# A transformer stack on one core: bias read backwards, low halves signalled by pairs, stage entries reordered

## The chip, the cores and the metric

The kernel runs on one core of one Trainium2 chip. The metric is the device time of one execution in microseconds. Before the change the median of three runs is 2583.01 us (2581.47 to 2585.11).

## What is computed

Two stacks follow each other on a sequence of 512 tokens of width 1024, batch 1, all in float32. The first has 16 meta tokens in front (528 columns) and two layers, `h = h + layer(rms_norm(h, g))`. The second has two rounds of feed-forward, mixer, feed-forward:

```python
def layer_ab(h, w_in, w_out, rel_bias, ...):  # layer 0: indexed sparse attention and gated linear attention
    z = h @ w_in
    # oa: softmax(q k + rel_bias[bucket(j - i)] + mask of the top-k scores) v, gated
    # ob: gated linear attention in chunks of 64, head norm, gated
    return jnp.concatenate([oa, ob], axis=-1) @ w_out

def layer_cd(h, w_in, w_out, ...):            # layer 1: retention and stick-breaking attention
    oc = head_layer_norm(retention_chunked(...)) * jax.nn.silu(cg)
    od = stick_breaking(...) * jax.nn.silu(dg)
    return jnp.concatenate([oc, od], axis=-1) @ w_out

for layer in range(2):                        # second stack
    x = x + 0.5 * swiglu(rms_norm_2(x, ffn1_norm[layer]), ...)
    hn = rms_norm_2(x, mix_norm[layer])
    x = x + (pool_mla_mixer(hn, ...) if layer % 2 == 0 else gated_conv_mixer(hn, ...))
    x = x + 0.5 * swiglu(rms_norm_2(x, ffn2_norm[layer]), ...)
```

with `swiglu(x) = (silu(x @ w_gate) * (x @ w_up)) @ w_down`, hidden width 2816, and `rms_norm(x, g) = x * rsqrt(mean(x * x) + 1e-6) * g`. The first stack ends in a further `rms_norm` with `final_g`.

## The kernel before

**State and blocks.** The activations stay transposed in SBUF as `H`: 128 channels on the partitions, 8 tiles (m or k = 0 to 7) of 528 or 512 tokens. All large products go through 219 weight blocks of 256 columns and up to 8 k-tiles of 128 rows (172 have 8, 24 have 4, 16 have 6). A block is loaded by SP into `raw` (two buffers, `load_block`, L443), rounded by ScalarE in one operation to its high half `wh` (`split_high`, L458), and POOL makes the low half `wl = raw - wh` in one operation for each two k-tiles (`split_low`, L468), up to four per block, and signals `weights_low` after the last. The activations are split in the same way into a high part `NH` by ScalarE and a low part `NL` by VectorE. TensorE then makes each product as three matmuls (high by high, high by low, low by high; `gemm_k`, L482). A block gives two output units of 128 rows and 512 columns (or two column halves of 264, line L493; or five token tiles, line L503), k running inside a unit.

**Order.** Every engine's order is written out by hand; engines wait for counting semaphores alone, in program order, so whatever stands behind a waiting instruction on an engine waits too. TensorE waits for the whole block's `weights_low` before its first unit. SP's loads wait until the block two before is consumed by POOL; `split_high` of block b waits until TensorE has finished block b - 2.

**PSUM.** Units without a bank of their own take bank `unit % 4`; `wait_slot` (L476) waits for the eviction of the unit that held the bank. Banks 4 to 7 serve the attentions, the sums of squares and the transposes.

**Entries.** The norm of a stage is put off: the products of a stage run on `H * g` and are scaled by 1/rms at eviction. So an entry into a stage (ab, cd, ffn0, mla, ffn1, ffn2, conv, ffn3) runs beside the end of the stage before. For each finished tile m VectorE adds the unit into `H` (L2320, L2322 or L1072), `late_act` (L563) makes the high part and the square on ScalarE, `late_dve` (L583) the low part (L590) and the sum of squares over tiles in `rstd` (L597; for ffn0 a second sum, weighted with `final_g`, in `both`, L596). `late_sum_pe` (L607) sums over the partitions on TensorE after the first unit of the new stage, and `late_root_act` (L623) and `late_scale_dve` (L636) make root and reciprocal (3.36 us for 512 columns on VectorE). `split_high` of the new stage's first two blocks stands among the `late_act` calls on ScalarE's queue (`out_tail_act` L2328, `ffn_act` L1028).

**Start.** SP loads the meta tokens, the constants, block 0, the four tiles of x, block 1 and small tables. TensorE transposes the meta tokens, then the gain rows (ten DMAs on ScalarE's queue), then x (32 transposes, L2530); ScalarE and VectorE evict them into `H`. The first two blocks run in two halves of k, so that they can begin before all input tiles are split.

**Bias of the sparse attention.** A line of 655 relative-position biases per head is written to HBM and read back with overlapping rows into `strip` (128 rows, each shifted by one). The rows come out mirrored over the partitions, and `strips_pe` (L1749) turns them with a matmul against `flip`, one head at a time in two column halves; `strips_act` (L1758) evicts them. POOL adds strip and mask into `bm` (L2382), VectorE adds `bm` to the scores (L910). `soft_pe` (L812) runs the steps i of an attention: transposes of the probabilities (`turn`), the next scores, values, and `fill(i)`, which is a number of k-steps of other blocks put in to keep TensorE busy (8 for i = 0 and 1 in the sparse attention, 1 in the latent attention). VectorE's list (`soft_dve`) runs beside it, with one round of the top-k selection in each of the first steps.

## Time and profile before

| | |
|---|---|
| median of three runs | 2583.01 us |
| profiled execution | 2583.35 us, span 2581.5 us |
| TensorE busy | 2500.5 us, 97% |
| POOL / VectorE / ScalarE busy | 1074.2 / 1018.9 / 872.5 us |
| chain that ended last | 88% TensorE, 5% VectorE, 3% ScalarE, 2% POOL |
| weights' low halves on POOL (L473) | 794 operations of 1346 ns |
| mean DMA rate | 84 GB/s |

Busy time says which engine is full; here TensorE nearly is, and what it loses has to be looked up place by place: in the view of waits (what TensorE waited for and how often), in the chain of work around each such place, and in the order of time of one engine. Mean durations come from the view that groups instructions by line and shape. A matmul's recorded duration covers its latency; the pace is the distance between starts. PEclk is the granted share of TensorE's 2.4 GHz.

### The profile page before, as it was taken

What the parts mean: (1) busy time and instruction counts of PE and PEld (TensorE: products, weight loads), DVE (VectorE), ACT (ScalarE), POOL (GpSimd) and SP (SyncE); (2) the same over time, 40 slices, a digit from 0 to 9 for tenths busy, and PEclk for the clock granted to TensorE, in tenths of its full rate; (3) what the DMA queues carried; (4) which work ended last, traced back from release to release, by engine and by line L of the source; (5) the groups of instructions that cost most, each with busy time, mean ns of one, the idle gap of its engine ahead of it and who ended that gap; (6) DMA issues with size and microseconds to landing.
All of it is one profiled execution on the core that took longest, in us unless ns stands there. A gap on an engine that the chain in (4) does not pass through costs nothing.

```text
span 2581.5 us, 31377 instructions
## 1 busy us (share of the span) xinstructions
PE 2500.5 (97%) x13015; PEld 2058.3 (80%) x13015; DVE 1018.9 (39%) x1663; ACT 872.5 (34%) x1294; POOL 1074.2 (42%) x830
## 2 busy tenths in 40 slices
PE   7999899999989999999999999999999999999999
PEld 6899768876668888878678888788888788888887
DVE  3666345235573131357452221531222544422222
ACT  4423444336642222235542222322222322322221
POOL 3233244331145444443154444444444444444443
PEclk9999999999999999999999999999999999999999
DMA  4122103211033333222133333233232333232322
GB/s 134 58 74 72 47 23 107 82 50 33 25 101 98 98 98 98 82 80 64 34 98 98 98 99 98 90 100 102 86 102 89 102 98 98 94 102 86 103 89 82
DMA packets 215847, 217.73 MB, mean 84 GB/s; under 512 B 10599, under 2 KB 213090, under 8 KB 215706
## 3 DMA queue, kind: packets, MB, share of 16 engines
q1 hardware_dynamic: 215504, 215.68, 26.3%
q8 instruction: 103, 1.69, 0.3%
q14 instruction: 38, 0.31, 0.0%
q10 hardware_dynamic: 202, 0.06, 0.0%
HBM read 213.60 MB, written 2.12 MB: 84 GB/s over the span
## 4 chain that ended last, share of the span: by engine, by line
PE 88%; DVE 5%; ACT 3%; POOL 2%; issue 1%; DMA 1%; ACTq 0%; DVEq 0%; SPq 0%
PE ps L500 68%; PE ps L493 6%; PE ps L503 4%; PE ps L497 2%; POOL wl L473 2%; PE ps L828 2%; ACT wh L466 1%; PE ps L863 1%; PE ps L845 1%; DVE rstd L597 1%; PE ps L2097 1%; PE ps L1585 1%; PE ps L522 0%; DMA raw<-in_w_in_ab 0%; DVE NL L590 0%
## 5 line engine op out<-in xcount | busy, mean ns | idle before, releaser
L473 POOL TENSOR_TENSOR wl<-raw,wh 128x512 fp32r<-128x512 f32 x794 | 1044.3, 1346 | 1453.1 <-ACT wh L466 1453.0
L500 PE MATMUL ps<-NH,wh 128*128 128x512 f32 (+1 forms) x1824 | 718.6, 394 | 21.5 <-POOL wl L473 14.1
L500 PE MATMUL ps<-NL,wh 128*128 128x512 f32 (+1 forms) x1824 | 712.9, 391 | 0.0
L500 PE MATMUL ps<-NH,wl 128*128 128x512 f32 (+1 forms) x1824 | 712.1, 390 | 0.0
L466 ACT ACTIVATE wh<-raw 128x2048 fp32r<-128x2048 f32 (+4 forms) x219 | 380.6, 1738 | 462.3 <-PE ps L500 404.2
L500 PEld LDWEIGHTS ps<-NH,wh 128*128 128x128 f32 (+1 forms) x1824 | 343.4, 188 | 102.8 <-POOL wl L473 17.4
L500 PEld LDWEIGHTS ps<-NL,wh 128*128 128x128 f32 (+1 forms) x1824 | 343.3, 188 | 73.7 <-issue 1.7
L500 PEld LDWEIGHTS ps<-NH,wl 128*128 128x128 f32 (+1 forms) x1824 | 343.3, 188 | 73.2
L500 PE MATMUL ps<-GH,wh 128*128 128x512 f32 x824 | 323.1, 392 | 0.0
L500 PE MATMUL ps<-GH,wl 128*128 128x512 f32 x824 | 320.7, 389 | 0.0
L500 PE MATMUL ps<-GL,wh 128*128 128x512 f32 x824 | 320.7, 389 | 0.0
L1072 DVE SCALAR_TENSOR_TENSOR H<-ps,H 128x512 f32<-128x512 f32 x96 | 66.4, 691 | 327.3 <-PE ps L500 327.0
L1039 ACT ACTIVATE GH<-tmp 128x512 fp32r<-128x512 f32 x88 | 55.7, 633 | 375.0 <-DVE tmp L1065 375.0
L500 PEld LDWEIGHTS ps<-GH,wh 128*128 128x128 f32 x824 | 154.7, 188 | 33.0 <-issue 1.2
L500 PEld LDWEIGHTS ps<-GH,wl 128*128 128x128 f32 x824 | 154.7, 188 | 32.3
L500 PEld LDWEIGHTS ps<-GL,wh 128*128 128x128 f32 x824 | 154.7, 188 | 31.5
L1035 ACT ACTIVATE sg<-sg 128x512 f32<-128x512 f32 x88 | 55.6, 633 | 316.2 <-DVE sg L1056 316.2
L1056 DVE TENSOR_TENSOR sg<-ps,rstd 128x512 f32<-128x512 f32 x66 | 45.7, 692 | 236.5 <-PE ps L500 236.4
L1062 DVE TENSOR_TENSOR tmp<-ps,rstd 128x512 f32<-128x512 f32 x66 | 45.7, 692 | 211.9 <-PE ps L500 211.9
L1067 DVE TENSOR_TENSOR GL<-tmp,GH 128x512 fp32r<-128x512 f32 x88 | 73.4, 834 | 61.6 <-ACT GH L1039 61.6
L1065 DVE TENSOR_TENSOR tmp<-sg,tmp 128x512 f32<-128x512 f32 x88 | 90.1, 1024 | 3.0
L503 PE MATMUL ps<-wh,NH 128*128 128x256 f32 (+1 forms) x320 | 90.7, 283 | 0.3 <-ACT dv L1777 0.3
(416 smaller groups left out, 2958.7 us busy)
## 6 DMA issues: line engine op xcount, KB each, us to landing
raw<-in_ffn_w_gate SPq DMA_DIRECT2D x44, 1024.0 KB, 5.3
raw<-in_ffn_w_up SPq DMA_DIRECT2D x44, 1024.0 KB, 5.3
raw<-in_ffn_w_down SPq DMA_DIRECT2D x32, 1024.0 KB, 5.1
raw<-in_w_in_ab SPq DMA_DIRECT2D x16, 1024.0 KB, 5.5
raw<-in_w_in_cd SPq DMA_DIRECT2D x14, 1024.0 KB, 5.0
raw<-in_ffn_w_down SPq DMA_DIRECT2D x16, 768.0 KB, 4.4
raw<-in_c_w_in SPq DMA_DIRECT2D x12, 1024.0 KB, 5.2
raw<-in_w_out_ab SPq DMA_DIRECT2D x8, 512.0 KB, 3.5
```

What stands on the lines that cost most here:

```text
L466: nc.scalar.activation(wh[:, b % 2, 0:k, 0:w], raw[:, b % 2, 0:k, 0:w], ACT.Copy).then_inc(S("weights_high"), 1)
L473: ins = nc.gpsimd.tensor_tensor(wl[:, b % 2, ks, 0:w], raw[:, b % 2, ks, 0:w], wh[:, b % 2, ks, 0:w].bitcast(F32), ALU.subtract)
L493: last = nc.tensor.matmul(ps[0:m1 - m0, bank + h, 0:T // 2], w[:, s, k, m0:m1], x(k)[:, h * (T // 2):(h + 1) * (T // 2)], start=start, sto ...
L497: last = nc.tensor.matmul(ps[:, bank, 0:T // 2], w[:, s, k, m0:m0 + P], x(k)[:, c0:c0 + T // 2], start=start, stop=stop)
L500: last = nc.tensor.matmul(ps[0:m1 - m0, bank, 0:SEQ], w[:, s, k, m0:m1], x(k), start=start, stop=stop)
L503: last = nc.tensor.matmul(ps[0:n_tok, bank, 0:total], x(k)[:, c0:c0 + n_tok], w[:, s, k, 0:total], start=start, stop=stop)
L828: last = nc.tensor.matmul(ps[0:n, A.score_bank(i) + x, 0:min(w - 512 * x, 512)], A.q(h, c0, n), A.k(h, 512 * x, min(w - 512 * x, 512)), st ...
L1035: nc.scalar.activation(sg[:, i, :], sg[:, i, :], ACT.Silu).then_inc(S("gate_silu"), 1)
L1039: nc.scalar.activation(GH[:, 2 * p_ + i, :], tmp[:, i, 0:SEQ], ACT.Copy).then_inc(S("hidden_high"), 1)
L1065: nc.vector.tensor_tensor(tmp[:, i, 0:SEQ], sg[:, i, :], tmp[:, i, 0:SEQ], ALU.mult).then_inc(S("hidden"), 1)
L1067: nc.vector.tensor_tensor(GL[:, 2 * p_ + i, :], tmp[:, i, 0:SEQ], GH[:, 2 * p_ + i, :].bitcast(F32), ALU.subtract).then_inc(S("hidden_low" ...
L1072: nc.vector.scalar_tensor_tensor(out=H[:, m, META:T], in0=ps[:, bank_of(u), :], scalar=0.5, in1=H[:, m, META:T], op0=ALU.mult, op1=ALU.add ...
```

## The change

- **Strips.** The table of buckets is mirrored on the host, `flip` and both strip routines are gone, and each use reads `strip` backwards along its columns (step -1). TensorE waits only for the value units' evictions before the attention. SP loads block ag+1 ahead of the strip.
- **Signals per pair.** POOL signals `weights_low` after each pair of k-tiles, and TensorE waits in a block's first unit pair by pair.
- **Entries.** `late_act` and `late_dve` are cut into high part, square, low part and add. On ScalarE the split of the next blocks goes ahead of the squares, on VectorE the adds run a tile behind the low parts. Except in ab and cd the squares are written to PSUM banks 6 and 7 (and 4 and 5 for ffn0's second ones). ffn0's sum goes behind the second unit, and its second reciprocal behind the first two evictions.
- **Banks.** `unit % 4` becomes `(unit + 2) % 4`; kv_up and q_up follow.
- **Fill.** `fill(0)` runs ahead of step 0.
- **Start.** x is loaded ahead of block 0, and block 0 in two halves; the gain rows are transposed after x; ScalarE splits block 0 in two operations after its evictions; the squares of ab come after all high parts, their adds after all low parts.

```diff
-    out["flip"] = np.eye(P)[::-1]
-    return (np.arange(32)[:, None] == b[None, :]).astype(np.float32)
+    return np.ascontiguousarray((np.arange(32)[:, None] == b[None, ::-1]).astype(np.float32))
-            bank = b.bank[i] if b.bank else unit % 4
+            bank = b.bank[i] if b.bank else (unit + 2) % 4
@@ split_low
         for k0 in range(0, k, 2):
+            if b == 0 and k0 % 4 == 0:
+                pool.wait_ge(S("weights_high" if k0 else "first_high"), 1)
             ks = slice(k0, min(k, k0 + 2))
-            ins = nc.gpsimd.tensor_tensor(wl[:, b % 2, ks, 0:w], ..., ALU.subtract)
-        ins.then_inc(S("weights_low"), 1)
+            nc.gpsimd.tensor_tensor(wl[:, b % 2, ks, 0:w], ..., ALU.subtract).then_inc(S("weights_low"), 1)
@@ unit_steps, gemm
-            pe.wait_ge(S("weights_low"), b + 1)
             wait_slot(pe, BLOCKS[b].unit0 + i)
             for k in range(BLOCKS[b].kts):
+                if i == 0 and k % 2 == 0:
+                    pe.wait_ge(S("weights_low"), low_count(b, k))
                 gemm_k(pe, b, i, k, hi, lo)
-            if i == 0 and sums:
+            if sums and i == (sums == "ffn0"):
                 late_sum_pe(pe, sums)
@@
+    def late_square_at(name, m):
+        return tmp[:, m % 2, 0:T] if name in ("ab", "cd") else ps[:, 6 + m % 2, :]
+    def late_pair_act(act, name, q, b):
+        late_high(act, name, 2 * q)
+        if q:
+            late_square(act, name, 2 * q - 1)
+        if q < KT // 2 - 1:
+            split_high(act, b)
+            late_high(act, name, 2 * q + 1)
+            late_square(act, name, 2 * q)
+        else:
+            late_high(act, name, KT - 1)
+            split_high(act, b)
+            late_square(act, name, KT - 2)
+            late_square(act, name, KT - 1)
@@ late_scale_dve, ffn_dve
             step(dve, nc.vector.reciprocal(both[:, :], both[:, :]))
-            dve.wait_ge(S("norm_root"), roots_before[name] + 2)
+            return
+                    if p_ == 0:
+                        dve.wait_ge(S("norm_root"), roots_before["ffn0"] + 2)
+                        step(dve, nc.vector.reciprocal(rstd[:, 0:SEQ], rstd[:, 0:SEQ]))
@@ soft_pe
         scores(1)
+        A.fill(0)
         for i in range(N):
-            if A.fill:
+            if i:
                 A.fill(i)
@@ strips
+    def strip_of(h, at_, n, w):
+        a = strip[0:n, h, T - 1 - at_:T - at_]
+        return bass.AP(a.tensor, a.offset, [list(a.ap[0]), [-1, w]])
-            return strip[0:n, h, 400:400 + w]
+            return strip_of(h, 400, n, w)
-        strips_pe(pe)
-        pe.wait_ge(S("strip_out"), HEADS)
+        pe.wait_ge(S("evac_act"), evacs_before(FIRST["ag"], "A"))
@@ out_tail_dve (ffn_dve in the same manner, without the lag of the low part)
             if m:
-                late_dve(dve, after, m - 1)
-        late_dve(dve, after, KT - 1)
+                late_low(dve, after, m - 1)
+            if m >= 2:
+                late_add(dve, after, m - 2)
+        late_low(dve, after, KT - 1)
+        late_add(dve, after, KT - 2)
+        late_add(dve, after, KT - 1)
@@ sync
-        load_block(sp, 0)
         for t in range(NT):
             sp.dma_start(xt[:, t, :], inp["x"][0, t * P:(t + 1) * P, :]).then_inc(S(f"x_in_{t}"), 16)
+        for h in range(2):
+            src = inp["w_in_ab"][0][h * D // 2:(h + 1) * D // 2, ...].rearrange("(k p) c -> p k c", p=P)
+            sp.dma_start(raw[:, 0, 4 * h:4 * h + 4, :], src).then_inc(S("raw_ready_0" if h else "raw_first"), 16)
+        load_block(sp, FIRST["ag"] + 1)
         sp.wait_ge(S("bias_stored"), 16)
         sp.wait_ge(S("gla_mix_low"), NT + 1)
         sp.dma_start(strip[:, :, :], ...)
@@ scalar
-        split_high(act, 0)
         for t in range(NT): ...                # evictions of x
+        split_first_high(act, 0)
         act.wait_ge(S("gain_done"), 1)
-        late_act(act, "ab", 0)
-        late_act(act, "ab", 1)
+        late_high(act, "ab", 0)
+        late_high(act, "ab", 1)
+        split_first_high(act, 1)
+        late_high(act, "ab", 2)
+        late_high(act, "ab", 3)
         split_high(act, 1)
-        for m in range(2, KT):
-            late_act(act, "ab", m)
+        for m in range(4, KT):
+            late_high(act, "ab", m)
+        for m in range(KT):
+            late_square(act, "ab", m)
```

## Rows read from the trace of the kernel before

**Rows 1.** the page's busy shares, and the chain of work: start us, us, what

```profile
PE 2500.5 (97%) x13015; PEld 2058.3 (80%) x13015; DVE 1018.9 (39%) x1663; ACT 872.5 (34%) x1294; POOL 1074.2 (42%) x830
...
1681.53 341.45 PE ps L500 x1506
```

**Rows 2.** TensorE's waits in the whole span: us in total, times, longest

```profile
PE ps L500 <- POOL wl L473: 15.1, 9, 2.6
```

**Rows 3.** the chain of work in the first 48 us

```profile
10.84 5.36 PE ps L2530 x32
...
34.72 11.29 PE ps L500 x48
```

**Rows 4.** the instructions on tile xt, with first and last start in us

```profile
L2342 SPq DMA_DIRECT2D xt<-in_x x4: 432/513/1067, 2.1 to 3.7; - x4
...
DMA to landing us min/median/max: 7.6/8.8/10.0
```

**Rows 5.** TensorE in order of time: start us, us, instruction [idle before, releaser]

```profile
18.39 0.47 PE L500 MATMUL ps<-NH,wh 128*128 128x512 f32 x1 [2.20 <-DVE NL L590]
18.70 0.40 PE L500 MATMUL ps<-NL,wh 128*128 128x512 f32 x1
```

**Rows 6.** by line and shape: count | busy us, mean ns | idle before

```profile
L473 POOL TENSOR_TENSOR wl<-raw,wh 128x512 fp32r<-128x512 f32 x783 | 1034.9, 1352 | 1436.1 <-ACT wh L466 1436.1
...
L466 ACT ACTIVATE wh<-raw 128x2048 fp32r<-128x2048 f32 x170 | 324.2, 1907 | 419.7 <-PE ps L500 367.2 <-PE ps L493 40.1 <-PE ps L497 9.2
...
L597 DVE TENSOR_TENSOR rstd<-rstd,tmp 128x512 f32<-128x512 f32 x42 | 47.2, 1123 | 0.0
...
L2322 DVE TENSOR_TENSOR H<-ps,H 128x512 f32<-128x512 f32 x24 | 16.5, 687 | 35.1 <-PE ps L500 31.9 <-PE ps L522 3.1
...
L2382 POOL TENSOR_TENSOR bm<-strip,score 128x528 f32<-128x528 f32 x8 | 10.9, 1358 | 12.4 <-DVE mx L910 12.4
```

**Rows 7.** chain, then TensorE and VectorE in order of time, around the strips

```profile
249.93 11.53 DMA raw<-in_w_in_ab
...
259.56 1.94 PE L1755 MATMUL ps<-strip,K 128*128 128x264 f32 x8
265.36 8.21 PE L1755 MATMUL ps<-strip,K 128*128 128x264 f32 x24 [3.86 <-ACT strip L1762]
...
275.58 0.52 PE L493 MATMUL ps<-NH,wh 128*128 128x264 f32 x2
...
282.67 0.48 PE L493 MATMUL ps<-NH,wh 128*128 128x264 f32 x2 [0.72 <-DVE agT L1746]
...
276.65 0.69 DVE L1691 MAX8 top<-score 128x8 f32<-128x528 f32 x1
```

**Rows 8.** VectorE and TensorE in order of time, entry into cd

```profile
413.44 0.71 DVE L2320 TENSOR_TENSOR H<-ps,H 128x528 f32<-128x528 f32 x1 [0.92 <-PE ps L493]
...
420.75 1.79 DVE L590 SCALAR_TENSOR_TENSOR NL<-H,gain,NH 128x528 fp32r<-128x528 f32 x1
422.46 1.79 DVE L597 TENSOR_TENSOR rstd<-rstd,tmp 128x528 f32<-128x528 f32 x1
...
424.35 1.19 PE L614 MATMUL ps<-K,rstd 128*16 128x1 f32 x10
```

**Rows 9.** the chain of work, entry into ffn0

```profile
720.79 5.93 PE ps L500 x24
...
762.20 3.36 DVE both L645
...
778.80 1.43 PE ps L500 x5
```

**Rows 10.** chain at ffn1 and ffn2, and ffn1's window: busy us, PEclk, DMA

```profile
1311.36 7.31 PE ps L500 x24
...
1674.92 5.76 PE ps L500 x24
...
1311.00:1315.00 4.00, 3.64 (x9) 2.89 (x10) 4.00 (x3) 2.33 (x3) 4.00 (x4) 0.57 0.58 172
```

More of the change, by code:

```diff
@@ L192, in weight_plan @@
         blocks.append(Block(("a_w_in_2", 0), (0, D), cols, "DD"))
[L193 to L194 removed]
+    add("kv_up", "a_w_kv_up_2", 0, 0, 256, 0, 1024, "A", "T0", [2, 3, 0, 1] * 4)
+    add("q_up", "a_w_q_up_2", 0, 0, 384, 0, 768, "A", "T0", [2, 3, 0, 1] * 3)
     add("out_pool", "a_w_out_2", 0, 0, D // 2, 0, D, "D", "F", [2, 3, 2, 3, 2, 3, 2, 3])
@@ L237, in bank_of, with low_count @@
     return UNITS[u][2]
+LOW_BEFORE = [0]
+for _blk in BLOCKS:
+    LOW_BEFORE.append(LOW_BEFORE[-1] + -(-_blk.kts // 2))
+def low_count(b, k):
+    return LOW_BEFORE[b] + k // 2 + 1
 def program(nc, inp, const_in, buckets_in, out, bias_line):
@@ L544, in gemm @@
             for k in range(blk.kts):
+                if i == 0 and k % 2 == 0:
+                    pe.wait_ge(S("weights_low"), low_count(b, k))
                 if i == 0 and ready:
@@ L595, in late_dve @@
             if name == "ffn0":
-                nc.vector.tensor_tensor(both[:, :], both[:, :], sg[:, m % 2, :], ALU.add)
-            ins = nc.vector.tensor_tensor(rstd[:, 0:w], rstd[:, 0:w], tmp[:, m % 2, 0:w], ALU.add)
+                nc.vector.tensor_tensor(both[:, :], ps[:, 4 + m % 2, :], both[:, :], ALU.add)
+            ins = nc.vector.tensor_tensor(rstd[:, 0:w], late_square_at(name, m), rstd[:, 0:w], ALU.add)
             if name == "ffn0" and m == KT - 1:
@@ L603, in late_dve @@
             if name == "ffn0":
-                nc.vector.tensor_copy(both[:, :], sg[:, 0, :])
-            nc.vector.tensor_copy(rstd[:, 0:w], tmp[:, 0, 0:w]).then_inc(S("square_added"), 1)
+                nc.vector.tensor_copy(both[:, :], ps[:, 4, :])
+            nc.vector.tensor_copy(rstd[:, 0:w], late_square_at(name, 0)).then_inc(S("square_added"), 1)
     def late_sum_pe(pe, name):
@@ L1074, in ffn_dve @@
                 if t0 == GROUPS[-1][0] and AFTER[f]:
-                    late_dve(dve, AFTER[f], m)
+                    late_low(dve, AFTER[f], m)
+                    if m:
+                        late_add(dve, AFTER[f], m - 1)
+            if t0 == GROUPS[-1][0] and AFTER[f]:
+                late_add(dve, AFTER[f], KT - 1)
     def ffn_pe(pe, f):
@@ L1747, in ab_dve @@
                                        in1=halves(rstd[0:n, :], T), op0=ALU.mult, op1=ALU.mult).then_inc(S("evac_dve"), 1)
-    def strips_pe(pe):
-        pe.wait_ge(S("side_in"), 32)
-        for h in range(HEADS):
-            if h >= 2:
-                pe.wait_ge(S("strip_out"), h - 1)
-            for x in range(2):
-                last = nc.tensor.matmul(ps[:, 2 + 2 * (h % 2) + x, 0:halfT], const("flip"), strip[:, h, x * halfT:(x + 1) * halfT], start=True, stop=True)
-            last.then_inc(S("strip_turned"), 1)
-    def strips_act(act):
-        nc.scalar.preload_act_table_set("natural_log_exp_and_others")
-        for h in range(HEADS):
-            act.wait_ge(S("strip_turned"), h + 1)
-            nc.scalar.activation(halves(strip[:, h, :], T), banks(2 + 2 * (h % 2), T), ACT.Copy).then_inc(S("strip_out"), 1)
     def cd_name(b):
@@ L2355, in _ @@
         sp.dma_start(strip[:, :, :], bass.AP(bias_line.tensor, bias_line.offset, [[1, P], [BIAS_SPAN, HEADS], [1, T]])).then_inc(S("side_in"), 16)
-        for b in range(FIRST["ag"] + 1, C0 + 2):
+        for b in range(FIRST["ag"] + 2, C0 + 2):
             load_block(sp, b)
@@ L2381, in _ @@
                 pool.wait_ge(S("unit_done"), units_before(OG))
-            nc.gpsimd.tensor_tensor(bm_of(i)[:, 0:w], strip[:, h, at_:at_ + w], score[:, SCO[t - 1]:SCO[t - 1] + w], ALU.add).then_inc(S("bias_masked"), 1)
+            nc.gpsimd.tensor_tensor(bm_of(i)[:, 0:w], strip_of(h, at_, P, w), score[:, SCO[t - 1]:SCO[t - 1] + w], ALU.add).then_inc(S("bias_masked"), 1)
             if i in (9, 15, 23, 31):
@@ L2454, in _ @@
         nc.vector.tensor_copy(H[:, :, 0:META], ps[:, 4, 0:KT * META].rearrange("p (k n) -> p k n", k=KT)).then_inc(S("h_done"), 1)
-        dve.wait_ge(S("gain_turned"), 1)
-        nc.vector.tensor_copy(gain[:, 0:NROWS], ps[:, 0, 0:NROWS]).then_inc(S("gain_done"), 1)
         for t in range(NT):
@@ L2459, in _ @@
             nc.vector.tensor_copy(H[:, 0:4, META + t * P:META + (t + 1) * P], ps[:, 4 + (2 * t + 1) % 4, :].rearrange("p (k n) -> p k n", k=4)).then_inc(S("h_done"), 1)
+        dve.wait_ge(S("gain_turned"), 1)
+        nc.vector.tensor_copy(gain[:, 0:NROWS], ps[:, 0, 0:NROWS]).then_inc(S("gain_done"), 1)
         for m in range(KT):
-            late_dve(dve, "ab", m)
+            late_low(dve, "ab", m)
+        for m in range(KT):
+            late_add(dve, "ab", m)
         dve.wait_ge(S("gain_done"), 1)
@@ L2517, in _ @@
         last.then_inc(S("turned_in"), 1)
-        pe.wait_ge(S("rows_in"), 16 * len(ROWS))
-        nc.tensor.transpose(ps[:, 0, 0:NROWS], rows[:, :], ident[0:NROWS, 0:NROWS]).then_inc(S("gain_turned"), 1)
         for g in range(2 * NT):
@@ L2531, in _ @@
             last.then_inc(S("turned_in"), 1)
+        pe.wait_ge(S("rows_in"), 16 * len(ROWS))
+        nc.tensor.transpose(ps[:, 0, 0:NROWS], rows[:, :], ident[0:NROWS, 0:NROWS]).then_inc(S("gain_turned"), 1)
         pe.wait_ge(S("gain_done"), 1)
```

60 lines of the change are left out of this document (31 added, 29 removed).

## The prediction

> **What bounds the kernel now.** I read the profile in this order: busy shares, who waits for whom on TensorE, then the chain of work at each place with a wait. TensorE is busy 97% of the span of 2581.5 us, and in the long dense stretches one 512-column matmul follows another every 341.45/1506 = 0.2267 us [rows 1]. The change takes away hardly any of that arithmetic, so all it can gain is TensorE's waits, the stretches in which it runs at half clock, and the 32 flip matmuls. TensorE's waits are short and many: the longest sum is that on the low halves of the weights from POOL, 15.1 us in 9 waits, none over 2.6 [rows 2]. The reader should see that the eight entries into a new stage hold nearly all of them, and that between the entries there is nothing to gain.
>
> **Part 1, the start (inputs first, block 0 in halves, squares put off).** Before, the x tiles land 7.6 to 10.0 us after issues at 2.1 to 3.7, so at 9.7 to 13.7, 1.33 us apart, behind the 1 MB of block 0 [rows 4]. Moved ahead of it they land earlier by what that megabyte takes: two x tiles' worth is 2.7 us, and up to 4 if its small pieces are slower than x; the last x tile lands at 9.7 to 11.0. TensorE no longer waits for the gain rows in front of x either. It needs 5.36 us for the 32 transposes [rows 3], about what the landing takes, so it ends at 11.3 to 12.0 instead of 16.2: 4.5 us earlier. The gain transpose and its copy then stand behind x and ahead of the first product (0.7 us). New in front of the first product is the first half of block 0 on ScalarE (half of 1.907 us [rows 6], so 1.0) and POOL's first pair (1.35 [rows 6], up to 1.7 beside VectorE); the low part of input tile 0 runs beside POOL and takes up to 1.8, as the low parts of rows 8 do. So 12.0 + 0.6 (last eviction) + 1.0 + 0.7 (high part) + 1.5 = 15.8 for the first matmul, against 18.39 [rows 5]: 2.6 us. With the squares and their adds put off VectorE makes only low parts; one each 1.75 us against TensorE's 1.4 us per input tile of a block leaves four waits of 0.3 and 0.1 of others, where before there were two of about 1.8 and several of 0.1 (the end of the stage is 34.72 + 11.29 = 46.0 [rows 3], 27.6 us after the first matmul, for 96 matmuls of 0.23 and 1.6 us of bias line). That is 2.9 more: **-5.5** (-3.5 if x lands late, -7.2 if VectorE and POOL don't meet). The adds end near 33 us and the sum is wanted at 40, so the put-off squares are hidden here. The gain DMAs on ScalarE's queue, the rest of SP's queue and the load of block 2 (0.3 to 4 us later, because block 0's low half ends later) are hidden by block 0 and 1.
>
> **Part 2, the strips.** Before, 32 flip matmuls and eight evictions stand between the last value block (259.56) and the first fill (275.58): 16.0 us, of which 3.86 is a wait, because ScalarE is held by block ag+1, which lands 11.53 us after its issue behind the strip DMA [rows 7]. The clock falls in that wait: the last 24 flips take 8.21 us, the first 8 only 1.94 [rows 7]. After, the strip is read backwards where it is used, and block ag+1 is loaded before the strip, long before it is wanted. What remains is the wait for the last value eviction and two small score products, 1.3 us: -14.7. The moved fill gives part back. Fill 0 (5.95 us) now runs before turn 0, and fill 1 needs VectorE's eviction of fill 0's unit, which stands behind the copy of turn 0, logits 2 and one top-k round (0.69 + 0.09 + 0.69, each with its gap, 1.55 [rows 7]), all now late because they wait for turn 0; with the eviction of 0.71 fill 1 starts near 269.7, where it was 282.67 [rows 7]. **-12.9** (-10 to -14.7). POOL's reads with step -1 are not shown by any row; the adds are 1.36 us at most [rows 6] in steps of 3 us with one step of slack, so the bounds are 0 and, at three times the price, 1 us in each of the 8 widest, +8; I take 0, the row as it stands, since the number of elements is the same.
>
> **Part 3, signals per pair and the new order at the entries.** A block's low halves are four POOL operations, 5.9 us when VectorE is busy too, behind 1.9 us on ScalarE: 7.9 us after the last reader of the buffer; the block before it lasts 5.5 us at depth 4. With a signal per pair TensorE needs 1.9 + 1.5 = 3.4 us, and each later pair comes 1.5 us after, against 2.7 us of matmuls. At the depth-6 blocks in front of mla, ffn2 and conv (8.2 us) it is enough that the split stands ahead of the squares. So POOL's 15.1 us [rows 2] go, entry by entry:
> - mla, ffn2, conv: 1.9 each (the entry unit is 5.76 us [rows 10]). What is late next is the sum: last tile's eviction 0.75, high 0.65, split 1.9, two squares 1.3, then one add of 0.7 and two hand-overs, 5.4 us after the last unit, against 5.44 for the first unit of the new stage. It just fits, because the squares now lie in PSUM: an add with one PSUM operand takes 0.687 us even beside POOL (mean of 24), one with both in SBUF 1.123 on the mean of 42 [rows 6], and 1.79 beside POOL [rows 8]. -5.6, and -1.65 for the third block of mla's input, which is the same wait again.
> - ffn1: its wait of 2.6 us is followed by a stretch at 0.57 clock, so that 24 matmuls take 7.31 us instead of 5.6 [rows 10]. Both go, less 0.1: -4.2. ffn3: -0.3.
> - ffn0: two units from 720.79 are 5.5 us; eight units of 2.78 end at 743.4, two blocks of 10.9 and the two sums at full clock (1.7) with 0.7 for a late low part bring the third block at 768, where it was 778.80 [rows 9]. Putting the sum behind the second unit, both square sums in PSUM and the second reciprocal (3.36 [rows 9]) behind the first evictions make that reachable: sum at 755.3, root, one reciprocal, silu, split and pair end near 766.5, under the 768. **-10.9** (-8 if low parts beside POOL cost 1.8 each, -11.5).
> - cd: here the squares stay in SBUF and the split stands ahead of the last two. Before, VectorE has a queue without a gap from 413.44 to 424.25, and TensorE's sum starts just behind it at 424.35 [rows 8]. After, one more add lies behind the seventh tile and the last two squares come 2 us later: split ends 420.9, squares 422.1, two adds of 1.75: 425.0. TensorE has done its first unit by 421.8, so 2.4 us won become a wait of 3.2, +0.8. Waits of 2.6 and 3.86 us are followed by half clock [rows 7, 10]; I take 1.7 us for that: **+2.6** (-2.4 if VectorE keeps up, +4.5).
> - mla attention: one fill step (0.7 us) goes under the wait for the first exponentials: -0.7 (0 to -1.2).
> - Bank rotation: an entry's first units take the banks of four units before instead of two; no row waits for a bank there, 0.
> - The added waits are 575 on TensorE (one per pair instead of one per block). In the unit of [rows 10] eight satisfied waits leave 5.76 us for 24 matmuls, 23 steps of 0.2267 and one duration of 0.5, so 0 each; 0.005 at most, +3.
>
> The Trainium skill's page "SBUF — State Buffer", section "SBUF: two separate sides", says that a VectorE operation with two SBUF inputs and a GpSimd operation exclude each other for the whole instruction. The durations 0.69 and 1.79 agree. By that rule a blocked add costs up to a whole POOL operation of 1.35 more, 2.05, which would put 0.5 us on cd and make the sum -38.9. It speaks against splitting weights just when cd's adds run.
>
> **The sum**: -5.5 - 12.9 - 5.6 - 1.65 - 4.2 - 0.3 - 10.9 + 2.6 - 0.7 = **-39.2 us**. The profiled execution took 2583.35 us, 1.85 around its span; the median of the runs is 2583.01. So 2544.2 for that execution and 2543.8 for the median.
>
> **The rivals.**
> (a) The wait moves: the put-off squares end after the first unit at every entry. Then POOL's place is taken by the sum. If a PSUM operand spared nothing, each of five entries would wait 2 us (+10) and ffn0's six late adds would give back 4: 2558. A milder form (1 us each, half clock after two) gives +8: 2552. For it: cd's queue. Against: 0.687 us. Chance 0.15.
> (b) Slower: a satisfied wait on TensorE is not free. It decides from 39.2/575 = 0.068 us each. After a real wait the second matmul comes 18.70 - 18.39 = 0.31 us later instead of 0.23 [rows 5]; at 0.1 per wait the change costs 57: 2601. Against it stand the eight waits of rows 10. Chance 0.03.
> (c) The edits do more: cd's adds keep up (-5), fill 1 doesn't wait (-1.8), start -7: 2535. Chance 0.17.
> (d) The edits at the start and at the strips don't do what they say: x lands as late as before because its place in the queue doesn't set when it lands (-2 instead of -5.5), or reading backwards is three times as dear (+8): 2547 to 2555. Chance 0.10.
>
> **How the numbers follow.** Forecast 0.55, between 2540 and 2549 by the bounds of cd, ffn0 and the start; (a) 0.15, (b) 0.03, (c) 0.17, (d) 0.10. To leave out no more than 2 in 10 the range takes all of (d), the milder (a) and the upper half of (c): 2536 to 2555. A measurement of this kernel can tell 0.2% (5 us) from no change. Of the cases (b) alone is slower; with what I may have missed, faster 0.95, same 0.02, slower 0.03.
>
> **What would show it.** x transposed by 12 us and the first product near 15.8; no flip matmuls and full clock from 260 to 283; fill 1 waiting 2 us for VectorE; no wait on POOL at an entry; cd's sum waiting 3 us with half clock after it; ffn0's third block 11 us nearer to the stage's start; 0.2267 us per matmul in the dense stretches. A longer step there, or waits for the sum at mla, ffn1, ffn2 and conv, would make the prediction wrong.

## The result, and the profile after

The changed kernel takes 2541.89 us (median of four runs, 2540.93 to 2543.49), the kernel before 2582.98 beside it: a ratio of 0.9841, with a 95% interval from 0.9824 to 0.9858. That is 41.1 us less; the prediction said 39.2 less and 2543.8. The profiled execution has a span of 2540.6 us, against 2581.5. Times of variants below are medians of three to five executions; one execution of the variant with the warm start took 3108.64 us at a granted clock of 0.75 and is left out.

First TensorE's waits in the whole span (columns as in [rows 2]). The nine waits on POOL, 15.1 us, are gone, and only one has taken their place at an entry, the 2.4 us at the sum of cd. Of the waits that are left, the one for the constants at the very start (4.6 us, before 4.4) and the four at L2153 in stick-breaking (6.5 together, before 6.8) stand outside the change. Three single ones are what the rest of this text comes back to: 3.5 in front of the first product, 1.9 at fill 1, 2.4 at the sum of cd.

```profile
PE ps L2153 <- DVE soft_lo L2250: 6.5, 4, 1.9
...
PE ps L516 <- DVE NL L624: 3.5, 1, 3.5
PE ps L509 <- DVE agT L1797: 2.7, 3, 1.9
PE ps L653 <- DVE rstd L636: 2.4, 1, 2.4
```

The page and the chain of work of after. TensorE's busy time fell by only 11.9 us, to 98% of the span. The dense stretch is as dense as in [rows 1]: 359.09/1584 = 0.2267 us per matmul, with the added waits in it.

```profile
PE 2488.6 (98%) x12983; PEld 2053.7 (81%) x12983; DVE 999.4 (39%) x1663; ACT 866.2 (34%) x1287; POOL 1069.4 (42%) x830
...
1642.86 359.09 PE ps L516 x1584
```

The chain of work at the start of after, and the landing of the x tiles (answer to [rows 3 to 5]). x lands 4.3 to 6.9 us after its issues, where it was 7.6 to 10.0; the transposes end at 12.23, the first product starts at 15.85, and the first 48 matmuls take 13.90 us.

```profile
6.03 6.20 PE ps L2576 x32
...
14.45 1.27 DVE NL L624
...
15.85 13.90 PE ps L516 x48
```

```profile
DMA to landing us min/median/max: 4.3/5.6/6.9
```

Windows of after (busy us of PE, PEld, DVE, ACT, POOL with their instructions, then PEclk, DMA share, GB/s). Right behind the first product, behind fill 1 and behind the sum of cd the granted clock is half (0.50, 1.2 GHz). In the last row, where the stick-breaking stage begins, it is full, which will matter below.

```profile
14.60:21.30 6.70, 5.45 (x13) 4.32 (x14) 6.70 (x5) 6.70 (x9) 6.70 (x5) 0.50 0.13 34
...
264.00:267.00 3.00, 2.84 (x13) 2.84 (x14) 1.66 (x7) 0.65 (x1) 0.00 (x0) 0.50 0.29 103
...
407.20:413.80 6.60, 6.60 (x22) 5.51 (x20) 2.01 (x3) 0.70 (x3) 2.14 (x2) 0.50 0.47 159
...
562.90:569.50 6.60, 6.41 (x39) 4.69 (x40) 4.67 (x12) 5.35 (x16) 3.11 (x3) 1.00 0.34 113
```

TensorE and VectorE of after at the strips (answer to [rows 7]). The flip matmuls are gone. Fill 0 runs from 255.3 to 261.3; fill 1 waits 1.92 us for the eviction of L1797, and before that eviction stand a copy, the logits and one top-k round (MAX8 and MATCH_REPLACE8), just as the prediction had it.

```profile
255.14 0.22 PE L867 MATMUL ps<-akT,aqT 64*16 64x16 f32 x4 [0.66 <-ACT av L1770]
...
261.86 0.69 DVE L1742 MAX8 top<-score 128x8 f32<-128x528 f32 x1
...
262.67 0.69 DVE L1743 MATCH_REPLACE8 score<-top,score 128x528 f32<-128x528 f32 x1
263.39 0.71 DVE L1797 SCALAR_TENSOR_TENSOR agT<-ps,rstd 128x528 f32<-128x528 f32 x1
...
264.16 0.81 PE L509 MATMUL ps<-NH,wh 128*128 128x264 f32 x2 [1.92 <-DVE agT L1797]
```

By line and shape (answer to [rows 6]). The square sums at 512 columns take 681 ns, where they took 1123. The bias adds that read the strip backwards take 1357 ns, where the forward ones took 1358.

```profile
L636 DVE TENSOR_TENSOR rstd<-ps,rstd 128x512 f32<-128x512 f32 x42 | 28.6, 681 | 5.7 <-ACT ps L602 5.1
...
L2423 POOL TENSOR_TENSOR bm<-strip,score 128x528 f32<-128x528 f32 x8 | 10.9, 1357 | 12.4 <-DVE mx L950 12.4
```

The chain at the entry into ffn0 (answer to [rows 9]): 144 matmuls without a break, the four sum matmuls, and 353.65 us without a break. Second unit, square sums, root and reciprocal delay nothing.

```profile
704.48 33.54 PE ps L516 x144
738.02 0.86 PE ps L658 x2
738.88 0.86 PE ps L659 x2
739.74 353.65 PE ps L516 x1560
```

Where the time went: the start of the same TensorE instruction in both traces, and what each stretch gained (negative is faster).

| mark | before | after | difference | this stretch | predicted |
|---|---|---|---|---|---|
| index stage, second step | 63.77 | 59.99 | -3.8 | -3.8 | -5.5 |
| end of the value blocks | 259.56 | 254.48 | -5.1 | -1.3 | 0 |
| fill 1 | 282.67 | 264.16 | -18.5 | -13.4 | -12.9 |
| last spread of the sparse attention | 390.87 | 373.63 | -17.2 | +1.3 | 0 |
| cd, behind its entry | 461.86 | 447.76 | -14.1 | +3.1 | +2.6 |
| last suffix sums of stick-breaking | 660.54 | 644.24 | -16.3 | -2.2 | 0 |
| mla input, after the sum | 1124.78 | 1094.32 | -30.5 | -14.2 | -12.8 |
| latent projections | 1198.33 | 1166.09 | -32.2 | -1.8 | -1.65 |
| last spread of the latent attention | 1284.81 | 1252.11 | -32.7 | -0.5 | -0.7 |
| ffn1 | 1319.60 | 1282.80 | -36.8 | -4.1 | -4.2 |
| ffn2 | 1681.61 | 1642.92 | -38.7 | -1.9 | -1.9 |
| conv | 2043.59 | 2003.05 | -40.5 | -1.9 | -1.9 |
| ffn3, and to the end | 2219.09 | 2178.20 | -40.9 | -0.4 | -0.3 |

### The profile page after: what moved, and what is told of

Same layout as the page of the kernel before. It is cut to its first block, busy times and chain, and to the rows that moved or that the text cites. A ratio compares the mean times of both kernels' runs of the same rounds, so it can differ in the third digit from the quotient of the medians.

```text
span 2540.6 us, 31320 instructions
## 1 busy us (share of the span) xinstructions
PE 2488.6 (98%) x12983; PEld 2053.7 (81%) x12983; DVE 999.4 (39%) x1663; ACT 866.2 (34%) x1287; POOL 1069.4 (42%) x830
## 4 chain that ended last, share of the span: by engine, by line
PE 94%; DVE 3%; ACT 2%; issue 1%; DMA 0%; DVEq 0%; SPq 0%; ACTq 0%
PE ps L516 72%; PE ps L509 6%; PE ps L519 5%; PE ps L513 2%; PE ps L867 2%; PE ps L902 1%; PE ps L884 1%; ACT wh L475 1%; PE ps L2133 1%; PE ps L1636 1%; PE ps L538 0%; PE ps L1999 0%; PE ps L1979 0%; DVE rstd L636 0%; PE ps L2191 0%
## 5 line engine op out<-in xcount | busy, mean ns | idle before, releaser
L475 ACT ACTIVATE wh<-raw 128x2048 fp32r<-128x2048 f32 (+3 forms) x218 | 378.8, 1738 | 477.7 <-PE ps L516 425.2
```

What stands on the lines that cost most here:

```text
L475: nc.scalar.activation(wh[:, b % 2, 0:k, 0:w], raw[:, b % 2, 0:k, 0:w], ACT.Copy).then_inc(S("weights_high"), 1)
```

## The experiments

All are edits of the changed kernel, except where the kernel before is named, and the changed kernel's 2541.9 us is what they stand against. Each was timed beside the kernel before. The runs of one kernel lie 1 to 8 us apart, so each verdict rests first on the trace at its place, and the median stands beside it.

**The start: TensorE kept busy.**

```diff
+        for _ in range(16):
+            nc.tensor.transpose(ps[:, 1, 0:P], xt[:, 3, 0:P], ident)
         pe.wait_ge(S("gain_done"), 1)
         ready = late_ready(pe, "ab")
```

> The changed kernel with 16 transposes of an x tile into an unused bank between the gain transpose and the first product, so that TensorE isn't idle for 3.5 us there. Theory (the idle stretch from 12.3 to 15.85 us brings the half clock of 14.56 to 21.38, and that eats what the start should have gained): full clock from 11 us on, the first product still at 15.85, the first 48 matmuls in 10.9 us plus about 1 us of waits for low parts instead of 13.9; 2.0 us less than the changed kernel (2541.9), so 2539.9. Rival (the half clock is bound to the time since the start, or the low parts would have kept TensorE waiting all the same): 2541.9, first 48 matmuls 13.9 us as now.

TensorE at its first product, then the chain at the third input tile and windows of this kernel:

```profile
15.15 0.47 PE L516 MATMUL ps<-NH,wh 128*128 128x512 f32 x1 [1.79 <-DVE NL L624]
```

```profile
18.59 8.84 PE ps L516 x36
27.43 0.95 PE ps L2596 x2
```

```profile
13.80:20.40 6.60, 5.10 (x19) 3.34 (x20) 6.60 (x5) 6.32 (x8) 6.60 (x5) 1.00 0.30 89
559.30:565.80 6.50, 6.33 (x24) 3.96 (x25) 4.79 (x11) 5.32 (x16) 3.07 (x3) 0.50 0.38 115
```

The clock is full in the first window, and the first 48 matmuls take 27.43 - 15.15 = 12.3 us instead of 13.9: 1.6 less. But the time is 2542.12 us (2541.34 to 2542.57): the same as without the edit. The traces show two reasons.

First, the changed kernel's profiled run had drawn the dear case. Ten profiled runs, of the changed kernel and of nine variants, keep the idle gap of 3.5 us. Three of them have 6.8 us of half clock at the start (48 matmuls in 13.9 to 14.0 us), six have 3.4 us (12.7 to 13.0), and one, the variant further down that reads the strip forwards, has none (19.56 + 8.83 - 16.13 = 12.3 us). Its first product, then its chain and a window:

```profile
16.13 0.47 PE L516 MATMUL ps<-NH,wh 128*128 128x512 f32 x1 [3.54 <-DVE NL L624]
```

```profile
19.56 8.83 PE ps L516 x36
```

```profile
14.00:20.80 6.80, 4.53 (x17) 3.14 (x18) 6.07 (x4) 6.74 (x10) 6.65 (x5) 1.00 0.26 75
```

So half clock follows the gap in nine runs of ten, and in neither of the two runs (this one and the one with three edits) in which the gap is filled up to its last 1.8 us. That the idle stretch brings it is likely, but it doesn't bring it every time, and filling it is worth 0 to 1.6 us, 0.9 on the mean of the ten.

Second, half clock comes and goes elsewhere. At the beginning of stick-breaking, behind waits of 1.56 and 0.84 us that stand in both traces, this run has 6.8 us of half clock (the second window), and the changed kernel's profiled run has none (its window 562.90:569.50, the same work, above); in retention this run has 3.4 us less. Of the twelve profiled runs of the changed kernel and its variants, six show half clock at the beginning of stick-breaking, for 3.4 or 6.8 us, and six show none. The profiled run is 1.1 us shorter than the changed kernel's, and the medians can't tell the edit from nothing.

**Fill 1: the eviction ahead of the top-k round.**

```diff
@@ dsa_between
-        if eng is dve_e[0] and i <= LATE_ROUNDS:
-            next(dsa.rounds, None)
         for n, end in enumerate(DSA_ENDS):
             ...
+        if eng is dve_e[0] and i <= LATE_ROUNDS:
+            next(dsa.rounds, None)
```

> The changed kernel with VectorE's eviction of the fill units ahead of the top-k round in each step of the sparse attention instead of behind it. Theory (fill 1 waits 1.92 us because the eviction stands behind one top-k round of 1.5 us, and the half clock of 263.73 to 267.14 comes from that wait): the wait falls to 0.4 us, no half clock there, 1.5 + 1.7 = 3.2 us less: 2538.7. Rival (the round then makes the next probabilities late, and the wait moves to turn 1 or 2): 2541.9, the 1.9 us at another place of the same steps.

```profile
260.79 0.52 PE L509 MATMUL ps<-NH,wh 128*128 128x264 f32 x2 [0.38 <-DVE agT L1796]
```

```profile
262.00:266.00 4.00, 4.00 (x35) 4.00 (x34) 0.44 (x4) 0.50 (x1) 0.00 (x0) 1.00 0.21 74
```

In TensorE's timeline the wait is 0.38 us instead of 1.92, and the window behind it has full clock. From the first scores to the last spread the attention takes 115.5 us instead of 118.5, 3.0 less. Measured 2539.97 (2537.32 to 2540.76): 1.9 less. The theory holds, and no later turn waits longer.

**Fill 0 back behind turn 0**, as before the change.

```diff
         scores(1)
-        A.fill(0)
         for i in range(N):
             turn(i)
             ...
-            if i:
+            if A.fill:
                 A.fill(i)
```

> The changed kernel with fill 0 back behind turn 0 in both attentions. Theory (the moved fill covers the 3.1 us from the first scores to the first probabilities, 255.4 to 258.5, and gives 1.9 back as the wait of fill 1 for VectorE): 3.1 - 1.9 = 1.2 us more at the sparse attention, 0.7 more at the latent attention (its first wait 1.2 us again instead of 0.5), half clock in either: 2543.8. Rival (the move loses more than it covers, because the eviction behind the round is its doing): 2541 or less.

```profile
260.30 0.19 PE L881 MATMUL ps<-K,lg 16*16 16x16 f32 x1 [3.20 <-ACT lg L1035]
```

TensorE's timeline shows the 3.20 us that the moved fill covers, and fill 1 waits 0.63 instead of 1.92. The half clock after it lasts from 259.2 to 266.0, twice as long as in the changed kernel, so the attention takes 2.8 us more, not 1.2; the latent attention takes 0.6 more. Measured 2547.20 (2544.69 to 2549.59), 5.3 more. The sign is the theory's, the size is not: 3.4 stand at the two places. The profiled run is 7.1 us longer; the rest of that is half clock elsewhere, at 61.2, 566.4 and 1139.8 us (3.4 us each), against 3.4 us less of it at cd.

**cd: the sum behind the second unit.**

```diff
-            if sums and i == (sums == "ffn0"):
+            if sums and i == (sums in ("ffn0", "cd")):
```

> The changed kernel with the sum of squares of cd behind the second unit of its first block, as ffn0 has it. Theory (VectorE's last two adds beside POOL end at 407.0, 2.4 us after TensorE's first unit, and that wait costs 3.4 us more as half clock from 407.09 to 413.92): the wait of 2.4 us and the half clock both go, 5.8 us less: 2536.1. Rival 1 (the half clock there is not due to the wait): 2.4 less, 2539.5. Rival 2 (root and reciprocal of 3.4 us, now 1.5 us later after the sum, hold up the evictions and so the banks of the third block): the gain is given back there, 2541 to 2542.

```profile
421.18 0.48 PE L509 MATMUL ps<-NH,wh 128*128 128x264 f32 x2 [1.99 <-DVE cqT L1837]
```

The wait of 2.4 and its half clock are gone, but TensorE now waits 1.99 us at the third block for VectorE's eviction of cd's first unit, with 3.4 us of half clock behind it. The stretch from the last spread to the mark of cd takes 72.2 us instead of 74.1. Measured 2539.09 (2538.26 to 2544.02), 2.8 less. The second rival has the mechanism right: the sum is what the evictions wait for, and a bank of the first block is what TensorE needs next. It had the whole gain given back, and 1.9 us are left at the place.

**cd: the last four squares in PSUM.**

```diff
     def late_square_at(name, m):
+        if name == "cd" and m >= 4:
+            return banks(4 + 2 * (m % 2), T)
```

> The changed kernel with the squares of cd's last four tiles in PSUM banks 4 to 7, which are free by then. Theory (the adds of 1.8 and 1.5 us beside POOL are what makes cd's sum late): adds of 0.7 us, the sum waits under 0.3 us instead of 2.4, no half clock from 407 to 414: 5.8 us less, 2536.1. Rival (the sum is late because its last squares stand behind the split on ScalarE, whatever the adds cost): 0.9 us of wait or more is left, and half clock after it: 2539.5.

VectorE's last two adds, first of the changed kernel and then of this one, and a window of this one over the sum:

```profile
403.93 3.06 DVE L636 TENSOR_TENSOR rstd<-tmp,rstd 128x528 f32<-128x528 f32 x2 [0.74 <-ACT tmp L602]
```

```profile
401.65 1.52 DVE L641 TENSOR_TENSOR rstd<-ps,rstd 128x528 f32<-128x528 f32 x2 [0.23 <-ACT ps L607]
```

```profile
404.00:412.00 8.00, 8.00 (x43) 6.82 (x43) 5.22 (x7) 1.59 (x4) 2.29 (x2) 1.00 0.56 184
```

Two adds beside POOL take 1.52 us together, where they took 3.06. TensorE doesn't wait at all, the clock stays full, and the stretch takes 68.45 us instead of 74.13: 5.7 less, as the theory had it. The median is 2539.93 (2538.27 to 2543.24), only 2.0 less; the profiled run has gained 4.1 and again shows the half clock at stick-breaking (556.1 to 562.9) and 3.4 us of it at 460.5, where the changed kernel's had none.

**Where the squares lie, in all entries.** Here every square goes to `tmp`, and ffn0's second ones to `sg`.

```diff
     def late_square_at(name, m):
-        return tmp[:, m % 2, 0:T] if name in ("ab", "cd") else ps[:, 6 + m % 2, :]
+        return tmp[:, m % 2, 0:T if name in ("ab", "cd") else SEQ]
```

> The changed kernel with all squares of the late norms in SBUF (as cd has them), nothing else. Theory (an add with one operand in PSUM takes 0.68 us even beside POOL, one with both in SBUF up to 1.8; the sums just fit because of that): L636 between 0.7 and 1.8 us each, up to 1.1 us more wait for the sum at each of mla, ffn1, ffn2, conv, ffn3, and 2 at ffn0: 2 to 8 us more, 2546 as the middle. Rival (a PSUM operand spares nothing, or there was slack): adds as now and 2541.9.

Waits on TensorE, the adds by shape, and the chain at ffn1, of this kernel:

```profile
PE ps L659 <- DVE rstd L636: 10.0, 5, 2.8
```

```profile
L636 DVE TENSOR_TENSOR rstd<-tmp,rstd 128x512 f32<-128x512 f32 x42 | 48.8, 1161 | 6.5 <-ACT tmp L602 6.0
```

```profile
1281.33 1.70 DVE rstd L636
1283.03 0.61 DVE H L2358
...
1284.29 1.91 ACT wh L475
...
1286.75 1.37 DVE rstd L636
...
1288.22 1.58 DVE rstd L636
...
1289.84 2.08 PE ps L659 x2
```

Measured 2560.11 (2559.32 to 2560.57): 18.2 more, over twice the upper end of what I expected. TensorE waits for the sum 0.9 us at mla, 2.8 at ffn1, 2.4 at ffn2 and conv and 1.5 at ffn3, together 10.0, where it was at most 0.13 us late; ffn0 has two waits for low parts, 1.5 us together; and half clock of 3.4 us, worth 1.7, follows at ffn0, ffn1 and ffn2. That is 10.0 + 1.5 + 5.1 = 16.6. Two more such stretches stand at 186.9 and 1139.2, where nothing waits longer than before, and at the start and at cd the half clock is 3.4 us shorter each. The chain shows why it is more than the 1.1 us of one slow add. An add of 1.70 us delays the last tile's addition into `H`, that delays its high part and the split, and the last two adds stand behind them: three slow adds in one chain, not one. They take 4.65 us where three of 0.68 take 2.04, and that 2.6 us is nearly all of ffn1's wait of 2.8. This is rival (a) of the prediction turned on; its 2558 is 2 us from what was measured, though ffn0 lost about 4 us and the five sums waited 2 us only on the mean.

The Trainium skill's page "SBUF — State Buffer", section "SBUF: two separate sides", says that a VectorE operation with two inputs in SBUF and a GpSimd operation that reads SBUF exclude each other for the whole instruction. The rows agree: 0.67 to 0.69 us in all 42 adds with one input in PSUM, 0.68 to 1.81 with both in SBUF.

**The kernel before with its squares in PSUM**, and nothing else.

```diff
-        nc.scalar.activation(tmp[:, m % 2, 0:w], late_src(name, m), ACT.Square)
+        nc.scalar.activation(late_square_at(name, m), late_src(name, m), ACT.Square)
```

> The kernel before with one part of the change alone: the late squares in PSUM instead of SBUF, except in ab and cd. Theory (the 18 us that the changed kernel loses with squares in SBUF are worth little here, because at mla, ffn1, ffn2 and conv TensorE's wait on POOL in front of the first unit covers the late adds; only ffn0, where the sum is late already, gains): adds of 0.68 us, 2 to 6 us less than before, 2577 to 2581. Rival (the squares' place is worth its 18 us by itself): 2565.

```profile
PE ps L500 <- POOL wl L473: 12.6, 8, 2.3
```

Measured 2573.33 (2569.43 to 2574.50), a ratio of 0.9958 (0.9944 to 0.9971): 10 less. It lies between the two expectations. Eight of the nine waits on POOL stay, so at mla, ffn2 and conv the faster adds bring 0.45 us each; ffn1 gains 2.0, its wait 2.2 instead of 2.6 and without the half clock. From stick-breaking to ffn0's third block the run gains 7.6 us: the sum waits 0.71 instead of 3.12, the waits of 0.95 for POOL and 1.94 for a low part in front of it are gone, and so is the half clock of 755 to 762. With 0.5 at ffn3 that is 11.5 at the places of the edit; a half clock of 10.2 us at 63.9, where the kernel before had none, takes 4.5 back, and one stretch fewer behind it gives 1.5. The same placement is worth 10 us here and 18 in the changed kernel.

**TensorE waits for whole blocks again.**

```diff
-                if i == 0 and k % 2 == 0:
-                    pe.wait_ge(S("weights_low"), low_count(b, k))
+                if i == 0 and k == 0:
+                    pe.wait_ge(S("weights_low"), LOW_BEFORE[b + 1])
```

> The changed kernel in which TensorE waits for a block's whole low half before its first unit (outside the start), all else as changed. Theory (at depth 4 the pairs do it, since 7.8 us from the last reader to the last low half stand against 5.5 us of matmuls; at depth 6 the order of the split does it alone): about 2.5 us of wait and 1.7 us of half clock back at ffn1, up to the same at ffn0, 0 at mla, ffn2 and conv: 4 to 9 us more, 2548 as the middle. Rival 1 (the pair signals do all): 1.9 us back at each of mla, ffn2 and conv too, 12 to 15 more. Rival 2 (the order does all): 2541.9.

```profile
PE ps L516 <- POOL wl L490: 5.0, 2, 3.4
...
PE ps L516 <- DVE H L2356: 2.3, 1, 2.3
...
PE ps L516 <- issue: 2.2, 1, 2.2
PE ps L516 <- DVE H L2358: 2.1, 1, 2.1
```

Measured 2551.90 (2550.99 to 2554.76), 10.0 more. The waits are 2.3 at cd, 2.1 at ffn0, 3.4 at ffn0's third block, 1.6 at mla's third block and 2.2 at ffn1; the profile names three different releasers, but at each of these places TensorE starts 0.1 us behind the end of POOL's last pair (at ffn1 1284.41 behind 1281.36 + 2.95). At mla, ffn2 and conv there is none, so there the order of the split is enough. At cd the wait costs nothing, since the sum then waits 2.4 us less and the half clock behind it is gone too. The theory named ffn0 and ffn1 and missed the third blocks of ffn0 and mla and the wait at cd; its upper end was 9 us more.

**Squares ahead of the splits again**, pair signals kept.

```diff
@@ late_pair_act
+        late_high(act, name, 2 * q)
+        late_square(act, name, 2 * q)
+        if name in ("cd", "ffn0", "ffn1", "ffn3"):
+            split_high(act, b)
+        late_high(act, name, 2 * q + 1)
+        late_square(act, name, 2 * q + 1)
+        if name in ("mla", "ffn2", "conv"):
+            split_high(act, b)
```

> The changed kernel in which ScalarE makes each square right after its high part and splits the next block behind that, as before; pair signals, PSUM squares and VectorE's order stay. Theory (pair signals and order each do alone at depth 6; at depth 4 the pairs do it): no wait on POOL over 0.5 us at any entry, 2541 to 2543. Rival (the order is what takes the waits away): waits of 1 to 1.9 us on POOL at mla, ffn2 and conv again, 2546 to 2548.

No wait on POOL comes back at any entry, so the rival falls: either part alone takes away the waits at depth 6. Measured 2545.73 (2543.07 to 2546.27), 3.8 more and above the theory. Two waits of 0.82 and 0.70 us for low parts are new, at cd and ffn0, because there the high parts now stand behind two squares; 1.9 us more in the profiled run come with half clock from 564.5 us, where stick-breaking begins.

**Reading the strip forwards.**

```diff
     def strip_of(h, at_, n, w):
-        a = strip[0:n, h, T - 1 - at_:T - at_]
-        return bass.AP(a.tensor, a.offset, [list(a.ap[0]), [-1, w]])
+        return strip[0:n, h, T - at_ - w:T - at_]
```

> The changed kernel with the bias strip read forwards from the mirrored place, so that the bias added is another one and only the time is to be read. Theory (step -1 costs nothing: the 528-column adds took 1.3 us at the median in both kernels): L2423 and the steps of the sparse attention as they are, 2541.9. Rival (the 1.3 us that the attention took longer than before comes from the backwards reads): 1 us or more less, 2540.5, with shorter adds on POOL or shorter steps on VectorE.

```profile
L2422 POOL TENSOR_TENSOR bm<-strip,score x16: 1026/1302/1689, 320.2 to 363.0; 128x400 f32<-128x400 f32 x8, 128x528 f32<-128x528 f32 x8
```

The line gives min/median/max in ns; backwards they are 1032/1306/1685. The attention takes 118.7 us, backwards 118.5. Measured 2543.45 (2542.45 to 2549.95). Direction costs nothing that these numbers can show.

**Some 2600 waits more.**

```diff
-                if i == 0 and k % 2 == 0:
-                    pe.wait_ge(S("weights_low"), low_count(b, k))
+                pe.wait_ge(S("weights_low"), low_count(b, k))
```

> The changed kernel with a wait on the signal of the weights' low halves ahead of every k-step of every unit, not only each second one of a block's first unit: some 2600 waits more on TensorE, nearly all on a value that was reached long before. Theory (a satisfied wait is free): 2541.9 and 0.2267 us per matmul in the dense stretches, at most 0.005 us each, 2555. Rival (b of the prediction, 0.068 us each): 2720.

```profile
1641.01 359.09 PE ps L516 x1584
```

The same 359.09 us for the same 1584 matmuls, and 2542.69 us: 0.8 more, 0.0003 us for each added wait and within the scatter. Rival (b) falls.

**The three edits together**, those of the warm start, of the eviction and of cd's squares in PSUM, as shown above.

> The changed kernel with three edits: transposes that keep TensorE busy before the first product, the eviction ahead of the top-k round, cd's last squares in PSUM. Theory (the three places are independent; by the traces of the single runs 1.6 at the start, 3.0 at the strips, 5.8 at cd): 10.4 us less than the changed kernel, 2531.5. Rival (as in the run with the warm start alone, the clock falls at other waits instead, in the retention and stick-breaking stages): only 5 to 7 less, 2535 to 2537.

Measured 2534.29 us (2531.27 to 2536.32, five runs), a ratio to the kernel before of 0.9809 (0.9796 to 0.9823), and 0.9970 of the changed kernel's median. The profiled run has 2529.5 us of span, 11.1 less than the changed kernel's. By the marks of the table it is 2.2 less at the start, 3.0 at the strips and 5.7 at cd. The beginning of stick-breaking is at full clock in this run:

```profile
552.00:559.00 7.00, 7.00 (x42) 5.14 (x43) 5.19 (x12) 5.12 (x16) 2.85 (x2) 1.00 0.44 145
```

So the sum of the three shows in the profiled run, which is the fastest of the five, and 7.6 of it in the median, which lies between the theory's 2531.5 and the rival's 2535 to 2537. The slowest of the five runs is 4.6 us under the fastest of the changed kernel, so the gain is clear of noise. It is the fastest version here.

## Why the prediction was right, and where it was not

- **Part 1, the start.** x landed in 5.6 us at the median instead of 8.8, the transposes ended at 12.23 (predicted 11.3 to 12.0) and the first product came at 15.85 (15.8). The step "that is 2.9 more" failed in this run: it was 1.2 (59.99 - 15.85 = 44.1 us from the first product to the mark, before 63.77 - 18.39 = 45.4). What this step had wrong is the clock, and nothing else. The sum took full clock; what came was half clock from 14.56 to 21.38, at which one matmul takes 0.43 us and VectorE keeps up. In the two runs with full clock there, with the gap filled (57.67 - 15.15) and with the strip read forwards (58.63 - 16.13), the stretch takes 42.5 us, 2.9 less than before, and small delays for low parts like those of the sum are back, 0.3 us at the third input tile. The prediction had itself lengthened TensorE's idle time in front of the first product, from 2.2 us [rows 5] to 3.5, and applied the lesson of [rows 7] and [rows 10] (a wait, then half clock) everywhere but here. -3.8 instead of -5.5. That the earlier landing comes from the place in the queue is what the two traces suggest; no run takes the order of the loads back alone.
- **Part 2, the strips.** -13.4 against -12.9 at fill 1, its wait 1.92 against 2. Then 1.3 come back as half clock from 263.73 to 267.14. Among its signs the prediction had "full clock from 260 to 283"; that was wrong, and for the same reason. The cost of reading backwards, 0 with an upper bound of 8, is 0.
- **Part 3.** ffn2, conv and ffn1 came as predicted, to 0.1 us. That it "just fits" is true to within half a microsecond: the weight load of the sum is 0.33 to 0.55 us late in four places, 1.5 together, its matmul at most 0.13. That the PSUM operand is what makes it fit is shown by the 18 us. ffn0 with mla's entry gained 14.2 against 12.8. ffn0's third block starts at 750.5, 12.0 nearer instead of 10.9; the remaining 2.2, up to mla's sum, stand against 1.9. Part of the 1.1 is in the prediction's own sum: 720.79 + 8 x 2.78 is 743.0, not 743.4, and with two blocks, the sums and the low part that gives 767.2, not 768. Of the rest, the low part that it had waiting for 0.7 us beside POOL didn't make TensorE wait. "Against 2.7 us of matmuls" for a pair is misread as well: in a block's first unit a pair lasts 6 x 0.2267 = 1.4 us, less than the 1.5 that POOL needs. It does no harm, because the first pair is ready 2 us before TensorE wants it (3.4 against 5.5).
- **cd.** The wait was 2.40 where the sum had 3.2, and the half clock 6.8 us where it had half of that: +3.1 against +2.6. Two errors of opposite sign, so the nearness is luck (and the sum's own terms, 0.8 and 1.7, make 2.5). That slow adds beside POOL make the sum late is shown by the variant with the squares in PSUM. In the paragraph on the Trainium skill, two adds 0.26 to 0.3 us longer would make the sum -38.7, not -38.9.
- **Fill of the latent attention, ffn3, satisfied waits:** as predicted, to 0.2 us. The experiment bounds a satisfied wait far below the 0.005 us that I allowed. No wait for a bank shows in the changed kernel, but no run has the bank rotation alone.
- **Not in the sum.** -1.3 up to the strips and -2.2 in retention and stick-breaking come with two half-clock stretches fewer, each of 3.4 us and worth 1.7. Two windows of before, then one of after over the same work as the second (the one over the same work as the first is the last window at the top):

```profile
577.80:581.00 3.20, 3.20 (x15) 1.48 (x12) 2.37 (x4) 3.14 (x11) 2.25 (x2) 0.50 0.03 5
192.10:195.30 3.20, 3.20 (x15) 2.89 (x14) 2.84 (x8) 1.56 (x11) 0.00 (x0) 0.50 0.00 0
```

```profile
187.50:190.70 3.20, 3.20 (x34) 2.75 (x27) 2.04 (x7) 2.15 (x14) 0.00 (x0) 1.00 0.00 0
```

No edit but the bank rotation and the waits per pair touches these stages, and the variants show such stretches coming and going there, so I take these 3.5 us for chance; that is argued, not shown. They stand against the 1.3 given back at the strips, the 1.7 missing at the start and the 0.5 at cd; the total is 1.7 better than forecast because ffn0 with mla's entry and the strips brought 1.9 more. So the entries and the strips were forecast by the right mechanism, and that the total came within 2 us is in part luck: 3.5 us that no term held cancel 3.5 us of half clock that the sum had missed.

## What to carry to other kernels

When the first wait at a place is taken away, work out which queue ends next and by how much, operation by operation, since one slow operation can stand in the chain more than once; here the placement of a scratch tile decided over 18 of 41 us, and over 10 in the kernel before. Put a possible price in clock on an idle stretch in front of dense matmuls (here gaps of 1.9 us and more), whatever ends it, as a range and not as one number, since the same gap cost 0, 3.4 or 6.8 us of half clock in different runs; and move the waiting engine's own small work into it. Changes of two or three microseconds are best judged at their own place in the trace, since in the median half-clock stretches elsewhere come and go.

## What the runs showed of the hardware that was not expected

- The same stretch of work behind the same waits (1.56 and 0.84 us) runs at half clock for 6.8 us in one run and at full clock in another. By the record of the granted clock, half-clock time within the span was 34 us in the changed kernel's profiled run, 31 with the warm start alone and 17 with the three edits joined. Of the 14 us between the last two, 10 stood right behind the waits of 1.9 and 2.4 us that the joined kernel doesn't have.
- A wait of 2.0 to 2.4 us was followed by 3.4 us of half clock in some places, by 6.8 in others and by none in others again (2.27 us at cd in the kernel before, 2.31 at cd and 2.21 at ffn1 with the waits for whole blocks); one of 0.4 us by none. Even the gap of 3.5 us at the start was followed by none in one run of ten.
- A negative step on POOL's input costs nothing: 1357 ns against 1358.
